# RWKV key norms ahead of the projection copies, HGRN states ahead of the mixing, and chunk products of odd token tiles on crossed partition halves

## The reference

```python
kk = heads(k * k_k, RW_HEADS)
kk = kk / jnp.maximum(jnp.linalg.norm(kk, axis=-1, keepdims=True), 1e-12)
k = k * (1 + (a - 1) * k_a)
# per head and chunk, with g = cumsum(log_w), a = -kk, b = kk * a_h:
L_ab = pair(a_dec, b_inv, strict);  L_ak = pair(a_dec, k_inv, strict)
M_rb = pair(r_dec, b_inv, incl);    M_rk = pair(r_dec, k_inv, incl)
lhs = eye(64) - L_ab
W1 = triangular_solve(lhs, a_dec);  U0 = triangular_solve(lhs, L_ak @ v)
Q_eff = r_dec + M_rb @ W1;          Y_intra = M_rb @ U0 + M_rk @ v
P = W1.T @ b_dec + diag(exp(g_last));  D = U0.T @ b_dec + v.T @ k_dec
S_next = S @ P + D;                 y = Y_intra + Q_eff @ S.T
```

## Time and profile before

| | |
|---|---|
| median of 3 runs | 3105.27 us (3102.4 to 3106.46) |
| the profiled execution | 3102.91 us, span 3101.1 us |
| busy share of the span | PE 97%, PEld 79%, GpSimd 76%, VectorE 44%, ScalarE 20% |
| granted TensorE clock, mean | 0.992 |
| instructions | 47691 |

### The profile page before, as it was taken

The page is one execution under the profiler, slowest core; times in us unless marked ns, Lnnn a source line. Parts: engine busy times, 40 slices in busy tenths (PEclk is TensorE's granted clock), DMA queues, the critical chain, the costliest instruction groups (busy, mean ns, idle before and its releaser), DMA issues.

```text
span 3101.1 us, 47691 instructions
## 1 busy us (share of the span) xinstructions
PE 2999.5 (97%) x20178; PEld 2449.0 (79%) x20178; DVE 1362.0 (44%) x1765; ACT 635.1 (20%) x1031; POOL 2344.7 (76%) x1877
## 2 busy tenths in 40 slices
PE   8999999989999999999899999999999999999996
PEld 7888877777778888888788888777777788888884
DVE  4221233765637462211762213238565555622127
ACT  1000124643310020000310002354432100200021
POOL 8988796742259989988899987867331799898875
PEclk9999999999999999999999999999999999999998
DMA  4332242111113333333233323422110233333322
GB/s 135 101 102 96 89 129 69 51 50 34 30 55 95 122 102 102 96 101 95 89 96 103 100 96 95 121 61 58 37 36 23 69 101 124 100 104 95 96 88 88
DMA packets 201488, 266.60 MB, mean 86 GB/s; under 512 B 12305, under 2 KB 130429, under 8 KB 201277
## 3 DMA queue, kind: packets, MB, share of 16 engines
q1 hardware_dynamic: 194624, 243.51, 25.8%
q10 hardware_dynamic: 6652, 20.05, 1.7%
HBM read 257.22 MB, written 6.29 MB: 85 GB/s over the span
## 4 chain that ended last, share of the span: by engine, by line
PE 83%; POOL 8%; DVE 5%; issue 2%; ACT 1%; DMA 0%; POOLq 0%; SPq 0%; DVEq 0%; ACTq 0%
PE ps L852 70%; POOL w_lo L1178 4%; POOL w_hi L1175 4%; PE ps L404 1%; PE ps L422 1%; PE ps L416 1%; PE ps L1051 1%; PE ps L1029 1%; PE ps L1045 1%; PE ps L1058 1%; PE ps L899 1%; PE ps L1098 1%; PE ps L486 0%; DVE hT_lo L1674 0%; PE ps L381 0%
## 5 line engine op out<-in xcount | busy, mean ns | idle before, releaser
L1175 POOL TENSOR_TENSOR w_hi<-w_raw,zero 128x512 fp32r<-128x512 f32 (+2 forms) x936 | 1085.3, 1159 | 649.9 <-PE ps L852 607.9
L1178 POOL TENSOR_TENSOR w_lo<-w_raw,w_hi 128x512 fp32r<-128x512 f32 (+2 forms) x936 | 1286.6, 1375 | 73.2
L852 PE MATMUL ps<-hT_hi,w_hi 128*128 128x512 f32 (+1 forms) x2368 | 927.7, 392 | 14.1 <-POOL w_lo L1178 11.4
L852 PE MATMUL ps<-hT_hi,w_lo 128*128 128x512 f32 (+1 forms) x2368 | 905.7, 382 | 0.0
L852 PE MATMUL ps<-hT_lo,w_hi 128*128 128x512 f32 (+1 forms) x2368 | 905.5, 382 | 0.0
L852 PEld LDWEIGHTS ps<-hT_hi,w_hi 128*128 128x128 f32 x2368 | 443.9, 187 | 123.8 <-POOL w_lo L1178 21.8
L852 PEld LDWEIGHTS ps<-hT_hi,w_lo 128*128 128x128 f32 x2368 | 443.7, 187 | 89.2
L852 PEld LDWEIGHTS ps<-hT_lo,w_hi 128*128 128x128 f32 x2368 | 444.2, 188 | 84.4 <-issue 2.9
L1746 DVE TENSOR_TENSOR act_raw<-silu,ps 128x512 f32<-128x512 f32 x88 | 59.9, 681 | 616.9 <-PE ps L852 616.9
L852 PE MATMUL ps<-w_hi,aT_hi 128*128 128x512 f32 x704 | 274.6, 390 | 0.0
L852 PE MATMUL ps<-w_lo,aT_hi 128*128 128x512 f32 x704 | 273.9, 389 | 0.0
(11 more groups left out here) (305 smaller groups left out, 3530.5 us busy)
## 6 DMA issues: line engine op xcount, KB each, us to landing
w_raw<-in_w_in SPq DMA_DIRECT2D x104, 512.0 KB, 3.6
w_raw<-in_ffn_wg SPq DMA_DIRECT2D x176, 256.0 KB, 2.8
w_raw<-in_ffn_wu SPq DMA_DIRECT2D x176, 256.0 KB, 3.1
w_raw<-in_ffn_wd SPq DMA_DIRECT2D x88, 512.0 KB, 3.6
w_raw<-in_w_in SPq DMA_DIRECT2D x96, 128.0 KB, 2.3
w_raw<-in_w_out SPq DMA_DIRECT2D x16, 512.0 KB, 3.7
w_raw<-in_ple_gate SPq DMA_DIRECT2D x16, 512.0 KB, 3.7
ln_rows<-in_ln_g ACTq DMA_DIRECT2D x8, 512.0 KB, 3.9
```

The source lines that it names most:

```text
L852: ins = nc.tensor.matmul(o, l_, r_, start=first, stop=last, skip_group_check=into is not None)
L1175: nc.gpsimd.tensor_tensor(w_split[0][:, q, kk, 0:w], w_raw[:, r, kk, 0:w], zero[:, 0:1].to_broadcast([P, w]), ALU.add).then_inc(*step("w_h ...
L1178: nc.gpsimd.tensor_tensor(w_split[1][:, q, kk, 0:w], w_raw[:, r, kk, 0:w], w_split[0][:, q, kk, 0:w].bitcast(F32), ALU.subtract).then_inc( ...
```

## The change

1. On ScalarE `norms_keys(L, 0)` stands ahead of the clearing of `bm` and `km` and of the copies `rkv_inputs(L, 1)`; the clearing moves behind it. The three copies of `rkv_inputs(L, 0)` stand together ahead of `rates(L, 0)`.
2. On VectorE the HGRN states stand ahead of all three `lora_mix`. On TensorE `rates_pe(L, 0)` moves behind HGRN's attention; 11 and 17 fill blocks stand around the key norm product, where there were 9 and 18.
3. Two steps of `prepare_dve` go: the key's factor is a scale of ScalarE's square and of the later product, and `(a-1)*k_a+1` is one ScalarE step in `decays`. Two small VectorE steps a layer make the columns for it. For ft > 0 two empty steps stand in the generator ahead of the key norm's use.
4. Products of odd token tiles read one half of the partitions and write the other, so that four products of a group lie on four quadrants. What belongs to them (`xl`, `invT`, `rhs`) lies in the crossed half for odd tiles. Strips, the first half of each widening, the L_ak v product and the solve write two banks, of even and of odd tiles; VectorE and ScalarE read them in two steps. `ar` is transposed crossed for odd tiles, by products with the identity; the first strips make a crossed transpose of `bm` beside the straight one. P, Q and D products are reordered over four corners; inner outputs, second halves of the widenings and the chunk steps stay.

```diff
+            PLACES = [(hd, t, cp, cp ^ (t % 2)) for hd in range(2) for t in range(NT) for cp in range(2)]
...
                 for t in range(NT):
-                    ins = nc.tensor.transpose(b[:, t * P:(t + 1) * P], src(t), ident())
+                    cols = slice(t * P, (t + 1) * P)
+                    if crossed and t % 2:
+                        for cp in range(2):
+                            ins = nc.tensor.matmul(b[unit(1 - cp), cols], src(t)[:, unit(cp)], ident(), start=True, stop=True)
+                    else:
+                        ins = nc.tensor.transpose(b[:, cols], src(t), ident())
...
+            def first_strips():
...
+                for hd, t, cp, side in PLACES:
+                    eye = ident()[unit(cp), unit(cp)]
+                    u = HEAD * (NT * hd + t)
+                    ins = nc.tensor.matmul(b[unit(cp), u:u + HEAD], bm[unit(cp), hd, t, 0, :], eye, start=True, stop=True)
+                    if t % 2:
+                        ins = nc.tensor.matmul(b2[unit(side), parity_cols(hd, t)], eye, bm[unit(cp), hd, t, 0, :],
+                                               start=True, stop=True)
...
             def strips(lev):
...
-                for hd, t in UNITS:
-                    for cp in range(2):
-                        ins = nc.tensor.matmul(b[unit(cp), unit_cols(hd, t)], bm[unit(cp), hd, t, 0, :],
...
+                for hd, t, cp, side in PLACES:
+                    ins = nc.tensor.matmul(b[t % 2][unit(side), parity_cols(hd, t)], bm[unit(cp), hd, t, 0, :],
+                                           inv[unit(cp), NT * hd + t, :], start=True, stop=True)
...
             def widen(lev):
...
+                    b = two_banks("rwi", "rw_inv", lev)
+                    for hd, t, cp, side in PLACES:
+                        ins = nc.tensor.matmul(b[t % 2][unit(cp), parity_cols(hd, t)], invT[unit(side), NT * hd + t, :],
+                                               xl[unit(side), NT * hd + t, :], start=True, stop=True)
...
-            for hd in range(2):
-                pe.wait_ge(*after("rw_wu", L, ft, hd))
...
+            for odd in range(2):
+                pe.wait_ge(*after("rw_wu", L, ft, odd))
+            corners = ((0, 0), (1, 1), (0, 1), (1, 0))
+            for t in range(NT):
+                for cp, hd in corners:
+                    nc.tensor.matmul(pq_bank[cp][unit(hd), t * HEAD:(t + 1) * HEAD], xx[unit(cp), hd, t, 0:HEAD],
+                                     b_tok[unit(cp), t, unit(hd)], start=True, stop=True)
...
-            v.tensor_scalar(rw_kk[:, :], rkv[:, 1, :], parT[:, R_KK + ft:R_KK + ft + 1], None, ALU.mult).then_inc(*step("rw_kkr", L, ft))
-            yield
...
-            v.tensor_scalar(rw_k2[:, :], rw_a[:, :], 1.0, parT[:, R_KA + ft:R_KA + ft + 1], ALU.subtract, ALU.mult).then_inc(
-                *step("rw_made", L, ft, "ka"))
-            yield
...
+            v.tensor_tensor(rw_k2[:, :], rw_k2[:, :], rkv[:, 1, :], ALU.mult).then_inc(*step("rw_k2", L, ft))
...
+            if ft:
+                yield
+                yield
             now("rw_rn", L, ft)
...
+                nc.scalar.activation(rw_k2[:, :], rw_a[:, :], ACT.Identity, bias=parT[:, R_KA1 + ft:R_KA1 + ft + 1],
+                                     scale=parT[:, R_KA + ft:R_KA + ft + 1]).then_inc(*step("rw_ka", L, ft))
```

More of the change, by code:

```diff
@@ new lines, in first_strips @@
+            def first_strips():
+                b = take(("rwx", L, ft, 0, 0), ("rw_inv", L, ft, 0, 1))
+                b2 = take(("rwc", L, ft), ("rw_invT", L, ft, 0))
+                for hd in range(2):
+                    pe.wait_ge(*after("rw_mask", L, ft, 0, hd))
+                for hd, t, cp, side in PLACES:
[5 more added lines that the diff above has]
+                                               start=True, stop=True)
+                ins.then_inc(*step("rwx_done", L, ft, 0))
@@ L461, in rwkv_core_pe @@
                     pe.wait_ge(*after("rw_tok", L, ft, 0))
[L462 to L466, removed]
+                    b = two_banks("rwl", "rw_lakv", 0)
+                    for hd, t, cp, side in PLACES:
+                        ins = nc.tensor.matmul(b[t % 2][unit(side), parity_cols(hd, t)], km[unit(cp), hd, t, 0, :],
+                                               v_tok[unit(cp), ft % 2, t, unit(hd)], start=True, stop=True)
                     ins.then_inc(*step("rwl_done", L, ft))
@@ L477, in rwkv_core_pe @@
             advance(fill["last"])
-            pe.wait_ge(*after("rw_lakv", L, ft))
+            pe.wait_ge(*after("rw_lakv", L, ft, 0, 1))
             pe.wait_ge(*after("rw_tok", L, ft, 1))
             pe.wait_ge(*after("rw_invT", L, ft, top))
[L482 to L488, removed]
+            b = [take(("rwu", L, ft, odd), ("rw_wu", L, ft, odd)) for odd in range(2)]
+            last = {}
+            for hd, t, cp, side in PLACES:
+                c = P * (2 * hd + t // 2)
+                last[t % 2] = nc.tensor.matmul(b[t % 2][unit(cp), c:c + P], invT[unit(side), NT * hd + t, :],
+                                               rhs[unit(side), hd, t, :], start=True, stop=True)
+            for odd in range(2):
+                last[odd].then_inc(*step("rwu_done", L, ft, odd))
             advance(fill["solve"])
@@ new lines, in rwkv_core_pe @@
+            for odd in range(2):
+                pe.wait_ge(*after("rw_wu", L, ft, odd))
[4 more added lines that the diff above has]
+                                     b_tok[unit(cp), t, unit(hd)], start=True, stop=True)
+            for t in range(NT):
+                for cp, hd in corners:
+                    last[cp] = nc.tensor.matmul(pq_bank[cp][unit(hd), 256 + t * HEAD:256 + (t + 1) * HEAD], xx[unit(cp), hd, t, 0:HEAD],
+                                                bm[unit(cp), hd, t, 1, :], start=True, stop=True)
@@ new lines, in rwkv_core_pe @@
+            for cp in range(2):
+                last[cp].then_inc(*step("rwpq_done", L, ft, cp))
+            for t in range(NT):
+                for cp, hd in corners:
+                    nc.tensor.matmul(d_bank[cp][unit(hd), t * HEAD:(t + 1) * HEAD], b_tok[unit(cp), t, unit(hd)],
+                                     xx[unit(cp), hd, t, HEAD:P], start=t == 0, stop=False, skip_group_check=True)
+            for t in range(NT):
+                for cp, hd in corners:
+                    last[cp] = nc.tensor.matmul(d_bank[cp][unit(hd), t * HEAD:(t + 1) * HEAD], k_tok[unit(cp), t, unit(hd)],
+                                                v_tok[unit(cp), ft % 2, t, unit(hd)], start=False, stop=t == NT - 1,
+                                                skip_group_check=True)
@@ L522, in rwkv_core_pe @@
+            for cp in range(2):
+                last[cp].then_inc(*step("rwd_done", L, ft, cp))
             y_bank = [take(("rwy", L, ft, hd), ("rw_y2", L, ft, hd)) for hd in range(2)]
```

157 lines of the change are left out of this document (71 added, 86 removed).

## The result

The changed kernel takes **3064.5 us** (median of four, 3063.6 to 3072.6) against 3105.2 before: a ratio of 0.9876, 95% interval 0.9858 to 0.9894. It is faster by 40.7 us. The forecast was 3050: its direction and the range for all cases (3034 to 3078) held, the likeliest case's own range (3040 to 3062) was missed by 2.5 us, and 14 us of the 55 forecast are missing.

A forecast was written before the change was run, and what follows sets the result against it. TensorE was taken as the bound almost everywhere (busy 97% of the span), VectorE next in tiles 1 and 2. Head 21 us plus quadrants 34 us is 55; 3105.3−55 gives 3050 us, range for all cases 3034 to 3078.

The forecast's parts named there:

- Term A: Head of the RWKV part: two long TensorE waits per layer go, and slow-clock work behind them; 21 us, bounds 12 and 22.
- a reserve of 2 us, no wait: At the head, key steps end at about 660 and TensorE has fill work until about 662, so pairs don't wait.
- Term B: Products on four quadrants in the cores: 54 us less TensorE work, less returned waits and clock; 34 us, bounds 12 and 54.
- the 0.47: In the cores, a 64-wide product group on four quadrants takes 0.47 us instead of 0.94; 14 groups a core.
- What the waits give back: New TensorE waits for VectorE at the last inverse, levels 3 to 5 and tile 3: 8.2 us a layer, 16.4 in all.
- The 0.3 for core 3: Returned wait in tile 3, where VectorE, busy 19 us, has only the P and D banks and solve copies: 0.3 us.
- The clock (−4): New waits may bring TensorE's lower clock in two or three short stretches, 1.3 to 1.6 us each: −4 us.
- The rival of the clock: Waits in the cores lower TensorE's clock for long stretches; 150 us of it gives about 3125 us; 4 in 100.
- The issue pace: TensorE's own instruction pace limits, so four quadrants give 64-wide groups nothing; 3084 us; 12 in 100.
- The head keeps a wait: Squares come 3 us later than reckoned, the key norm product stalls the fill, half the head's gain is lost; 3061; 10 in 100.
- VectorE not being in the way: Nothing comes back as waits in the levels of the cores, so the quadrants give 50 us; 3034 us; 8 in 100.
- products of crossed halves one after another: Products crossing halves don't run together, strips are no shorter, waits eat the head's gain: no change; 3 in 100.

The follow-up runs named there:

- i_head_alone: The kernel before with parts 1 and 2 of the change alone, without part 3 and without quadrants: 3082.2 us (0.9933).
- g: The changed kernel without its part 3, head order and quadrants kept: 3051.2 us (0.9832).
- d: The changed kernel with the HGRN output step that frees the key norm product's bank ahead of the waiting key step: 3062.5 us (0.9865).
- c: The changed kernel with the last update of invT ahead of the norm's sum and the decayed r on VectorE: 3059.3 us (0.9854).
- h: The changed kernel without part 3 and with ar transposed in 64x64 blocks on four quadrants: 3052.7 us (0.9835).
- j: d with an edit meant to cut GpSimd's splits to 16 of 384 columns; it took hold of no split: 3063.0 us (0.9875).
- k: g with the fill block behind the first pairs put ahead of the two transposes that wait for VectorE's y: 3052.4 us (0.9837).
- l: k with three of the fill blocks left at the end of the cores put into core 3: 3053.3 us (0.9839).
- e: The changed kernel with all of ar transposed in 64x64 blocks on four quadrants into two banks: 3066.1 us (0.9879).

## Why the prediction was right in direction and 14 us too low

**Term A, the head (21 us): right for the head's order.** `i_head_alone` measures 20.5. Both long waits are gone, and the first pair group takes 1.10 us instead of 1.98. Some of the close match is luck, since two things that the term left out nearly cancel: the cores of i wait 1.0 us more than those of before, over both layers, and core 2 of layer 1, which before ran at a granted clock of 0.97 with TensorE busy for 51.1 us, is at 1.00 and 49.5 in i.

**Part 3 (priced at 5.6 us of return): the step that failed most.** The prediction charged it 2.2 us a layer for the last inverse, and 0.6 in tile 0 for the factor behind ScalarE's HGRN copies. Measured are 12.3 by the gains and 13.3 by the medians (11.2 and 12.9 without quadrants). In the waits, which sum to 13.8: the solve 5.7 us, xl in core 0 3.0 (1.5 a layer for the 0.6), the inverse's update 1.4 more, and 3.7 at the key norm product, for which the prediction had nothing. The prediction followed that product's *input* (the squares, which came in time) and left out its *bank*. Ahead of the first HGRN output VectorE draws a fixed number of steps from the generator, in the changed kernel by `for _ in range(3): next(first)`; with the scaled key (g's L619) gone from the generator, the third draw is the key step that waits for ScalarE's factor, and it came to stand ahead of the HGRN output that frees the bank. So "a reserve of 2 us, no wait" failed at a place that it didn't look at. The reserve itself, before the pairs, was gone too, by VectorE's five key steps: reckoned at 3.5 us, they took 6.8, and with the bank freed (d) the pairs still wait 1.0 us. The front of the same prediction had shown that effect for the last level; it was not looked for at the head. This account of part 3's cost adds up waits of one trace; edits tried the solve (c) and the bank (d) by themselves, xl and the inverse's update only together with the rest (g).

**Term B, the work (54 us): mis-sized by 8.5.** Cores of layer 0 by windows (layer 1 agrees within 0.3 us): `i_head_alone` has 199.4 us of busy PE in four cores and `g_old_key_steps` 176.7, 22.8 a layer, 45.5 in all. A row of each:

```profile
716.60:773.20 56.60, 53.82 (x951) 41.46 (x950) 38.88 (x70) 19.39 (x28) 16.80 (x15) 1.00 0.14 39
```

```profile
712.70:765.70 53.00, 48.04 (x973) 34.73 (x972) 39.37 (x80) 19.46 (x29) 17.23 (x15) 1.00 0.15 42
```

That is 5.7 us a core against 6.7. Summed from start to start over both traces, with waiting taken off, the 14 groups save 5.9 a core, not 6.6. A widening saves its 0.47 (0.98 us before, 0.52 after, to the start of the next group), but a strip group ahead of fill saves 0.42 (1.03 and 0.61) and the P, Q and D groups 0.42 in the mean (0.94 and 0.52): where work of another shape or a wait follows, the end of a group isn't covered by the next one. The solve saves its 0.86, the transposes cost 0.85, and the group of the first strips, which was to cost nothing, some 0.06; small losses at other seams make up the rest.

The 0.015 us from which the 0.47 came was misread as well: the four rows are three steps in 0.06 us, 0.02 each. The whole seam bears it out all the same, with 13 starts from 870.90 to 871.08 us.

**What the waits give back (16.4, of which 10.8 not by part 3): mis-sized by 4.** TensorE waits 10.2 us in the four cores of layer 0 in i and 17.5 in g: 7.3 a layer, 14.7 in all. The 0.3 for core 3 failed most: it waits 4.6 us against 3.0 in i. The prediction had taken VectorE's 19 us of 46 for room, but VectorE is behind in the first levels of *every* core, where it has four masks of 0.7 us and the first inverse to make. A half read costs more than assumed, too: VectorE's step had a median of 0.42 us and two halves are 0.28 each, so +0.14 for the 0.1. (The 0.35 us that the prediction cites there as the earlier trace rows stands in the earlier trace rows.)

**The clock (−4): did not come in the profiled execution, but it does in others.** The granted clock is 1.00 in all eight cores after, with waits of up to 1.7 us in them. In the traces of c, d, h, j, k and l it isn't. The solve of core 2 waits 1.7 us in d as in the changed kernel, and here the lower of the two levels follows (granted clock 0.51; the same stretch of time, first of d, then of the changed kernel):

```profile
805.30:808.80 3.50, 3.29 (x91) 2.59 (x93) 0.69 (x2) 0.81 (x2) 0.00 (x0) 0.51 0.51 150
```

```profile
805.30:808.80 3.50, 2.94 (x117) 2.31 (x113) 1.48 (x3) 1.09 (x2) 0.23 (x1) 1.00 0.57 154
```

In d the first two of the P, Q and D groups there start 0.88 us apart instead of 0.48. The traces show three such stretches in d's cores, two in c's and none in those of the changed kernel, of g and of i; c has the lower level from 826 to 833 us. That is part of what the executions of one kernel scatter by: c's two executions at a mean clock of 0.996 took 3057.2 and 3057.3 us, the other two, at 0.994 and 0.995, 3062.6 and 3061.3. The rival of the clock was also argued against with too little. The prediction named the 1.00 of tile 2 in layer 0, but the same tile of layer 1 in the kernel before had 0.97, in a stretch 1.3 us longer:

```profile
2317.00:2371.80 54.80, 51.17 (x937) 39.74 (x936) 34.08 (x69) 19.40 (x28) 10.36 (x8) 0.97 0.09 29
```

**The sum.** 55, less 0.5 (head), 8.5 (work), 3.9 (other returns) and 7.7 (part 3), and 4 more for the clock, is 38.4, or 39.4 with part 3 by the gains. Measured are 40.7; the 1.3 to 2.3 between them are within what one kernel's gains scatter by.

**The rivals.** The issue pace fell with the 0.47 us. *The head keeps a wait* (10 in 100, 3061) came nearest, and the key norm product does stall the fill, as it said; but the squares weren't late, the bank was, and the larger part of what part 3 cost lies in the cores. VectorE not being in the way fell with the waits above, and so did products of crossed halves one after another with the 0.47 us; the clock didn't fall for the long stretches that its rival needed.

## What to carry to other kernels

When a step is taken out of an engine's order that is drawn by count, write down what each later draw now holds, at every place that draws: what was saved here was two steps (0.48 us for the one shown) on an engine that had room, and what it cost was 11 to 13 us of TensorE's time, since later steps moved ahead of ones that TensorE waits for. For a product follow its bank as closely as its inputs. And before filling or shortening one of many small waits, look at the engine that is behind: four of the edits here (e, h, k, l) moved a wait or TensorE's work and gained nothing.

## What the runs showed of the hardware

Two things were not expected. **VectorE and GpSimd lengthen each other.** One line of VectorE over its eight runs in the changed kernel (min, median and max in ns), and the first of them with two splits of GpSimd beside it:

```profile
L668 DVE TENSOR_TENSOR b_inv<-rw_ss,rw_cs x8: 676/682/1311, 661.5 to 2333.1; 128x512 f32<-128x512 f32 x8
```

```profile
659.70 1.34 POOL L1206 TENSOR_TENSOR w_lo<-w_raw,w_hi 128x384 fp32r<-128x384 f32 x1
661.01 1.27 POOL L1203 TENSOR_TENSOR w_hi<-w_raw,zero 128x384 fp32r<-128x384 f32 x1
```

In the six runs with no GpSimd step beside it the step takes 0.68 us, in the two at the heads 1.31; the two splits of that shape take 0.82 and 1.01 us while VectorE stands still (at 656.00 and 656.91 of the kernel before) and 1.27 and 1.34 here. At the head of the kernel before VectorE did these steps while TensorE stood still and GpSimd was idle, 0.69 us each. A VectorE step that reads PSUM and has only one input in SBUF stays as it is: this one (mean 683 ns) has a split beside it in 36 of its 48 runs and never takes over 0.70 us:

```profile
L1801 DVE SCALAR_TENSOR_TENSOR h_tok<-ps,h_tok 128x512 f32<-128x512 f32 x48 | 32.8, 683 | 437.4 <-PE ps L880 437.4
```

 The five key steps from L659 on thus take from 657.43 to 664.25, 6.8 us, and not the 3.5 that the prediction reckoned with: removing the wait brought back the neighbour. The Trainium skill says the same (SBUF — State Buffer, "SBUF: two separate sides"): the port pair that the two engines share is held exclusively, and a VectorE step with two SBUF inputs counts against a GpSimd step that reads SBUF. The trace agrees, 1.31 being a VectorE step and a part of a split. That it is the cause was read from the two traces and not tried, since the run meant for it (j) changed nothing; what it would be worth stays open. At the pairs of g it is little: the steps are as long there, and the pairs wait 0.19 us.

**Four quadrants really are four.** One instruction every 0.015 us held for whole groups; the price is at the changes of shape: four 128-wide transposes take 0.60 us together, drain included, and 1.2 when every second one is cut in halves of columns.
